# The last layer norm of a two-layer decoder step: tokens from 256 on turned to rows by a diagonal product, with mean and offset as a two-row product

## The reference

```python
def _layernorm(x, g, b):
    xf = x.astype(jnp.float32)
    mu = jnp.mean(xf, axis=-1, keepdims=True)
    var = jnp.mean(jnp.square(xf - mu), axis=-1, keepdims=True)
    y = (xf - mu) * lax.rsqrt(var + LN_EPS) * g.astype(jnp.float32) + b.astype(jnp.float32)
    return y.astype(x.dtype)
...
        yp = _layernorm(ALPHA * yp + 0.5 * _swiglu(yp, ffn2_wi[l], ffn2_wo[l]), ln_g[l, 2], ln_b[l, 2])
        ys = _layernorm(ALPHA * ys + 0.5 * _swiglu(ys, ffn2_wi[l], ffn2_wo[l]), ln_g[l, 2], ln_b[l, 2])
```

## Time and profile before

| | us |
|---|---|
| median of 3 runs (1842.55 to 1844.22) | 1843.87 |
| the profiled execution, its own time | 1845.71 |
| the span of its trace | 1843.9 |
| last product of the down projection ends, from the span's start | 1822.3 |
| from there to the end of the span | 21.6 |

### The profile page before, as it was taken

One profiled execution on the slowest core, in us unless ns is written; L12 is line 12 of the kernel. 1 busy time (PEld: TensorE's weight loads), 2 busy tenths in 40 slices (PEclk: granted clock), 3 DMA queues, 4 the chain that ended last, 5 costly groups with the idle time before them and its releaser, 6 DMA issues.

```text
span 1843.9 us, 35847 instructions
## 1 busy us (share of the span) xinstructions
PE 1766.2 (96%) x14078; PEld 1692.4 (92%) x14078; DVE 1455.5 (79%) x2188; ACT 932.3 (51%) x1464; POOL 422.9 (23%) x312
## 2 busy tenths in 40 slices
PE   7999999999997798999999999999999899999997
PEld 7999999986964488999999989999999799999996
DVE  5988887675988537988887599888876898887875
ACT  4455563353357736555562375555523475556333
POOL 3100044271220546000043230000542320002430
PEclk9999999999999999999999999999999999999999
DMA  5663423236210242343323324343323223433231
GB/s 167 193 200 96 114 87 103 87 100 140 54 55 1 61 123 70 92 114 104 101 92 98 109 69 111 94 114 103 98 83 118 57 56 106 114 102 104 81 103 47
DMA packets 275473, 180.73 MB, mean 98 GB/s; under 512 B 9367, under 2 KB 271903, under 8 KB 274846
## 3 DMA queue, kind: packets, MB, share of 16 engines
q1 hardware_dynamic: 266071, 158.50, 30.1%
q0 software_dynamic: 2144, 13.04, 2.0%
q10 hardware_dynamic: 7150, 7.70, 1.8%
HBM read 169.56 MB, written 8.08 MB: 96 GB/s over the span
## 4 chain that ended last, share of the span: by engine, by line
PE 74%; DVE 16%; ACT 6%; issue 3%; DMA 1%; POOL 0%; SPq 0%; ACTq 0%; DVEq 0%; POOLq 0%
PE ps L1372 41%; PE ps L1251 15%; PE ps L1435 9%; PE ps L1495 2%; DVE w_lo L1956 2%; PE ps L1500 1%; DVE q_lo L2643 1%; ACT xf L752 1%; ACT xh L750 1%; ACT p_t L887 1%; PE ps L1272 1%; DVE w_lo L2536 1%; ACT sc L865 1%; DVE q_sum L2720 1%; DVE xf L2006 1%
## 5 line engine op out<-in xcount | busy, mean ns | idle before, releaser
L2807 POOL TENSOR_TENSOR hl<-hid_all,hh 128x520 fp32r<-128x520 f32 x56 | 98.1, 1784 | 748.6 <-ACT hh L1111 748.6
L1041 ACT CAST w_hi<-w_sum 128x1024 fp32r<-128x1024 f32 x160 | 168.0, 1050 | 114.4 <-DVE w_sum L2518 107.0
L2536 DVE TENSOR_TENSOR w_lo<-w_sum,w_hi 128x1024 fp32r<-128x1024 f32 x160 | 194.4, 1217 | 4.5 <-ACT w_hi L1041 4.5
L1251 PE MATMUL ps<-hh,w_hi 128*128 128x260 f32 x896 | 191.7, 284 | 2.0 <-DVE w_lo L1956 2.0
L1251 PE MATMUL ps<-hh,w_lo 128*128 128x260 f32 x896 | 189.2, 282 | 0.0
L1372 PE MATMUL ps<-t_hi,w_hi 128*128 128x260 f32 x640 | 161.6, 284 | 0.7 <-DVE w_lo L2536 0.3
L1372 PE MATMUL ps<-xh,w_hi 128*128 128x260 f32 x640 | 159.9, 282 | 0.8 <-DVE w_lo L2536 0.8
L1372 PE MATMUL ps<-t_hi,w_lo 128*128 128x260 f32 x640 | 160.6, 283 | 0.0
L1372 PE MATMUL ps<-xh,w_lo 128*128 128x260 f32 x640 | 159.4, 283 | 0.0
L1251 PEld LDWEIGHTS ps<-hh,w_hi 128*128 128x128 f32 x896 | 145.3, 188 | 2.9 <-issue 2.7
L1251 PEld LDWEIGHTS ps<-hh,w_lo 128*128 128x128 f32 x896 | 145.6, 188 | 0.2
(11 more groups left out here) (376 smaller groups left out, 5234.7 us busy)
## 6 DMA issues: line engine op xcount, KB each, us to landing
w_raw<-in_ffn_wi_dram SPq DMA_DIRECT2D x176, 512.0 KB
w_raw<-in_ffn_wo_dram SPq DMA_DIRECT2D x16, 1024.0 KB
w_raw<-in_ffn_wo_dram SPq DMA_DIRECT2D x32, 512.0 KB
w_raw<-in_ffn_wo_dram SPq DMA_DIRECT2D x16, 768.0 KB
w_raw<-in_attn_w_in_dram SPq DMA_DIRECT2D x8, 1024.0 KB
keys_scratch<-key_half POOLq DMA_DIRECT2D x2, 2048.0 KB, 8.5
w_raw<-in_attn_w_o_dram SPq DMA_DIRECT2D x4, 1024.0 KB
x_in<-in_x_prompt_dram ACTq DMA_DIRECT2D x4, 512.0 KB, 9.9
```

The lines of the kernel that those rows point to most:

```text
L1041: nc.scalar.copy(blocks(st, j)[1][0][:, x], w_sum[:, c % 2, x]).then_inc(s_sums_hi, 1)
L1251: mm = nc.tensor.matmul(ps[0:mc, bank + 2 * m + h, 0:HT], w[:, k, m, 0:mc], x(k)[:, h * HT:(h + 1) * HT], start=first and k == 0 and w is ...
L2536: nc.vector.tensor_tensor(lo[:, x], w_sum[:, (st.chunk + j) % 2, x], hi[:, x].bitcast(F32), ALU.subtract).then_inc(s_sums_lo, 1)
L2807: nc.gpsimd.tensor_tensor(hl[:, k, :], hid_all[:, k, :], hh[:, k, :].bitcast(F32), ALU.subtract).then_inc(s_hl, 1)
```

## The change

Tokens 0 to 255 keep their path (subtract, multiply, gain and offset, transposes), now on 256 columns. Tokens 256 to 519 are no longer normalised in `xf`. With x a token's row before the norm, m its mean, s the root of its variance plus epsilon, g and b gain and offset, the output is (x g - m g + s b) / s. It is made piece by piece in PSUM:

- `scaled(i, q)`: four products with the raw `xf` tile as the stationary operand and `gain_diag` (a diagonal 128 x 128 matrix of the gain) as the moving one give x g, already turned to rows of tokens.
- `centred(i, q)`: one product with two rows, `token_rows` (-m and s, 2 x 128) stationary and `gain_rows` (g and b, 2 x 512) moving, is added in the same PSUM bank.
- The copy out multiplies by 1/s, one value for each partition (`token_stat`).

The three groups i = 2, 3, 4 each take 128 tokens; group 4 is the last 128 tokens, of which the last 32 partitions are copied out and the last 8 stored. Mean and mean square come from `token_moments`: for each group one product of the sum (stationary) with a single column of `mean_ones`, so that they stand one token to a partition, 128 x 3. DVE and ACT make m, s and 1/s on these 128 x 3 values, PE turns the pairs (-m, s) to two rows by three transposes, and DVE copies them into `token_rows`. `gain_diag` is written by ACT (eight 128 x 128 copies with a scale) after the last weights of the down projection have been split, into freed weight space, and SP loads `gain_rows` there in two transfers. `first_output` goes, `stats` of half 1 goes, and `variance` and `normalise` and `affine` of half 1 go.

```diff
-            for n in range(2, len(Y_ACT)):
+            for n in range(len(Y_ACT)):
                 output(n)
...
+            def final_tail(n, st, first_free):
+
+                order = (range(KD), range(KD))
+                act.wait_ge(s_lo, st.chunk + KF + 10 + 3)
+                for d in range(KD):
+                    x = nc.scalar.activation(gain_diag[:, d, :], ident, ACT.Copy, scale=gain(n, d))
+                x.then_inc(s_col_root, 1)
+                warm(ACT.Sqrt)
...
+            def scaled(i, q):
+
+                for d in range(4):
+                    nc.tensor.matmul(ps[:, Y_BANK[i, q], d * P:(d + 1) * P], xf[:, 4 * q + d, y_tokens(i)], gain_diag[:, 4 * q + d, :],
+                                     start=d == 0, stop=False, skip_group_check=True)
+
+            def centred(i, q):
+
+                nc.tensor.matmul(ps[:, Y_BANK[i, q], :], token_rows[:, (i - 2) * P:(i - 1) * P], gain_rows[:, q * 512:(q + 1) * 512],
+                                 start=False, stop=True, skip_group_check=True).then_inc(s_tr, 1)
...
+                pe.wait_ge(s_in, 16 * 8)
+                pe.wait_ge(s_col_var, 4)
+                centred(2, 0)
+                centred(2, 1)
+                centred(3, 0)
+                scaled(3, 1)
+                centred(3, 1)
+                pe.wait_ge(s_y_act, 1)
+                scaled(4, 0)
+                centred(4, 0)
+                pe.wait_ge(s_y_dve, 1)
+                scaled(4, 1)
+                centred(4, 1)
...
+                last_residual(0)
+                last_sums(st, 0, 0)
+                last_sums(st, 0, 1)
+                variance(st, eps, 0)
+                normalise(st, 0, order, 0, KD - 2, 2 * P)
+                last_residual(1)
+                last_sums(st, 1, 0)
+                last_sums(st, 1, 1)
+                normalise(st, 0, order, KD - 2, KD, 2 * P)
...
-                nc.vector.tensor_copy(dst, src).then_inc(s_y_dve, 1)
+                dst, src, rstd = y_half(i, q)
+                if i < 2:
+                    nc.vector.tensor_copy(dst, src).then_inc(s_y_dve, 1)
+                else:
+                    dve.wait_ge(s_col_root, 3)
+                    nc.vector.tensor_scalar(dst, src, rstd, None, ALU.mult).then_inc(s_y_dve, 1)
```

More of the change, by code:

```diff
@@ L743, in root, with affine @@
                 nc.scalar.activation(moment(1, h), moment(1, h), ACT.Sqrt).then_inc(s_rstd, 1)
-            def affine(n, st, h, split, order, begin, end):
+            def affine(n, st, h, split, order, begin, end, tokens=None):
+                tokens = tokens or cols(h)
                 for at_ in range(begin, end):
@@ L1930, in _ @@
             left()
[L1931 to L1938, removed]
         @block.vector
@@ L1993, in last_sums, with normalise @@
                 ins.then_inc(s_total, 1)
-            def normalise(st, h, order, begin, end):
+            def normalise(st, h, order, begin, end, count=HT):
+                tokens = slice(h * HT, h * HT + count)
                 n = {}
@@ L1998, in normalise @@
                     if at_ < end:
-                        x = xf[:, order[h][at_], cols(h)]
-                        n[at_] = step(nc.vector.tensor_tensor(x, x, moment(0, h), ALU.subtract))
+                        x = xf[:, order[h][at_], tokens]
+                        n[at_] = step(nc.vector.tensor_tensor(x, x, moment(0, h)[:, 0:count], ALU.subtract))
                     if at_ == begin + 1:
@@ L2004, in normalise, with final_tail @@
                         done(n[at_ - 1])
-                        x = xf[:, order[h][at_ - 1], cols(h)]
-                        nc.vector.tensor_tensor(x, x, moment(1, h), ALU.mult).then_inc(s_t, 1)
+                        x = xf[:, order[h][at_ - 1], tokens]
+                        nc.vector.tensor_tensor(x, x, moment(1, h)[:, 0:count], ALU.mult).then_inc(s_t, 1)
+            def final_tail(st, eps, last_residual):
+                order = (range(KD), range(KD))
+                last_residual(0)
[7 more added lines that the diff above has]
+                normalise(st, 0, order, KD - 2, KD, 2 * P)
+                mean, square, var, inv = (token_stat[:, n, :] for n in range(4))
+                dve.wait_ge(s_col_sum, 2)
+                nc.vector.tensor_scalar(token_pair[:, :, 0], ps[:, 7, 0:3], -1.0, None, ALU.mult).then_inc(s_col_var, 1)
+                done(step(nc.vector.tensor_copy(mean, ps[:, 7, 0:3])))
+                done(step(nc.vector.tensor_tensor(square, mean, mean, ALU.mult)))
+                done(step(nc.vector.scalar_tensor_tensor(var, ps[:, 7, 3:6], eps, square, ALU.add, ALU.subtract)))
+                nc.vector.tensor_scalar(var, var, eps, None, ALU.max).then_inc(s_col_var, 1)
+                dve.wait_ge(s_col_var, 2)
+                nc.vector.reciprocal(inv, var).then_inc(s_col_var, 1)
+                dve.wait_ge(s_col_sum, 3)
+                nc.vector.tensor_copy(token_rows[:], ps[0:2, 7, 0:3 * P]).then_inc(s_col_var, 1)
             def tail(st, eps, last_residual, nxt, early):
```

100 lines of the change are left out of this document (83 added, 17 removed).

## The result

| | before | changed | forecast |
|---|---|---|---|
| median, us | 1843.67 (13 runs) | 1847.78 (13 runs) | 1840.6 (range 1838.6 to 1844.0) |
| range of the runs, us | 1840.05 to 1847.13 | 1844.65 to 1848.99 | |
| ratio to before, 95% interval | | 1.0020 (1.0012 to 1.0027) | 0.998 |
| span of the profiled execution, us | 1843.9 | 1846.1 | 1840.6 |
| end of the down projection to the end of the span | 21.6 | 24.7 | 18.3 |

The last row is the one to work with, and is called the tail from here on. A difference of whole times holds this variation, the tail doesn't.

A forecast was written before the change was run, and what follows sets the result against it. Late stores behind a serial chain set the old end; PE becomes the bound. From 1822.3, PE ends at 1837.05, copy 1837.75, issue 1837.8, landing 2.4 and end 0.4 give 1840.6 us, 3.3 less; range 1838.6 to 1844.0.

The forecast's parts named there:

- PEclk 1.00 throughout: Sign of a right forecast: PE at full clock from 1822.3 to about 1837 us, behind the down projection.
- the clock falls and stays low to the end: Rival: PE's path from 1826.8 us takes twice as long, +10.1 us, 1850.7 us, slower; chance 0.05.
- The weaker rival, low for 6.8 us and back: Rival: the clock falls behind the down projection as before, losing 3.4 us; 1844.0 us, no gain; chance 0.09.
- -3.3 as forecast: Forecast gain at the end of the span: 1840.6 us, 3.3 us less than 1843.9.
- the faster landing: Last store, 32 KB to HBM: 2.4 us (2.0 to 3.0) from issue, plus 0.4 us to the span's end.
- the prediction's own rule: In the clock rivals, PE work takes twice as long at PEclk 0.50, so half of a low stretch is lost.
- the rival of 0.53 us: Rival: `centred` products cost 0.53 us instead of 0.87, six times 0.34 less; 1838.6 us; chance 0.05.
- the one-column products: Six PE products turning the sums into moments, after three pieces of `scaled`: 0.20 us each, 1.2 us, ending at 1826.1.
- the chain on 128 x 3 values: Small operations, root, pair transposes and DVE copies before the first `centred`, until about 1828.9 us; PE was to cover them.
- the last piece of cover before `last_residual(1)`: Three more tiles ahead of it cost DVE 2.0 us of 2.86 us idle; free, with 0.8 us left.
- the stores spread: Store groups released near 1829.7, 1830.4, 1831.8 and 1834.5 us, 1.2 us each, leaving the queue empty for the last store.
- without gaps: Sign of a right forecast: PE busy without gaps from 1822.3 to about 1837 us.

The follow-up runs named there:

- with 128 rows: Changed kernel with the two rows of `centred` operands repeated 64 times over 128 rows, pair scaled; median 1840.26 us, ratio to before 0.9984; again 1839.81 us, 0.9987.
- the stretch of 120 transposes: Kernel before with gapless PE work added behind its end: runs of 512-column products on 128, 2, 32 and 64 rows, then 120 transposes; 1960.85 us.
- 64-row version: Changed kernel with the pair and the gain and offset rows repeated over 64 rows; median 1839.99 us, ratio to before 0.9974; again 1842.72 us, 0.9996.

## Why the prediction was wrong

Measured from the end of the down projection, in us:

| | forecast | changed kernel | with 128 rows |
|---|---|---|---|
| transposes begin | 4.5 | 4.6 | 4.6 |
| first `centred` begins | 6.8 | 6.9 | 6.9 |
| PE ends | 14.7 | 21.7 | 14.8 |
| SP issues the last store | 15.5 | 22.5 | 15.7 |
| the span ends | 18.3 | 24.7 | 17.9 |

**The step that failed** is the forecast's "PEclk 1.00 throughout": the products of `centred` are summed at the full clock, and the rival "the clock falls and stays low to the end" is put aside. Its mechanism was named, with "5.2 of the 7.8 us are products that use two rows of the array" as the reason for it, and given a chance of 0.05. It is what happened: PEclk 0.50 from 1831 on, and 12.05 us for the six pieces behind it where 5.2 (six times 0.87) had been forecast. The reason set against it, that the clock had come back at 1833.3 with nothing but sixteen transposes done, was a true reading of the earlier trace rows, and the stretch of 120 transposes bears it out; but it answers the half of the rival that concerns transposes, and says nothing of products on two rows. The trace of before has no product on two rows, which the prediction says where it costs `centred`, and then bounds its duration only, never its effect on the clock. But it has products on eight rows, and right behind them, at 416.8 us, a fall under a PE without a gap; the prediction read the clock at the end of the trace alone. The weaker rival, low for 6.8 us and back, had the greater chance (0.09) because it repeated what the trace of before had shown.

**The price** put on this rival, +10.1 us, was for a clock low from 1826.8 on. It fell at 1831, four microseconds later, and its moment is partly chance: the traces differ by 2.7 us in it, which is worth half of that in time. The part from there to PE's end takes 12.05 us; the same products take 6.44 us in the 64-row version at the full clock and 5.27 us in the 128-row one. So 5.6 us are the clock's and 1.2 us the cost of changing between few and all rows, which the prediction does not have. The sum against before: -3.3 as forecast, +5.6 and +1.2, +0.1 in the first three `centred`, +0.2 in small delays elsewhere, -0.6 for the faster landing: +3.2, and the tails give 24.7 - 21.6 = +3.1. By the prediction's own rule 12 us at the low clock lose 6 us of a gain of 3.3, which gives a small loss, as measured. That the medians lie 4.1 us apart, 1 us more than the tails, is variation ahead of the tail.

**The rest held.** `scaled` at 0.87 us a piece (24 records in 2.8 us ahead of the moments, the latency of the last included); `centred` at 0.87 us by columns (2.77 us for three, 0.86 with 128 rows), so the rival of 0.53 us is out; the one-column products 0.24 us instead of 0.20; no wait of PE for the chain on 128 x 3 values; the last piece of cover before `last_residual(1)` 0.9 us (0.8 forecast); PE the bound and the stores spread. PE did idle for 0.67 us ahead of the transposes, where the prediction's list of signs says "without gaps"; its own times (1826.1 and 1826.8) have that gap. With 128 rows the tail is 17.9 us, 0.4 less than forecast: the store takes 2.2 us from issue to the end of the span, in the changed kernel and in the 128-row one alike, where 2.8 was taken, and 0.2 us are lost ahead of its issue.

The Trainium skill, TensorE: Matmul & The Clock Gate, section "What's actually happening", has the clock follow how busy PE has been. Here PE was busy for all of 1830.50 to 1831.00 and of every window behind it, and the clock fell; it also fell twice in the gapless stretches. With busy read as the busy time of the profile, the forecast would have stood by that rule; the measurement decides. The same page's "Part 4: PE-mode transpose", which the prediction had weighed and set aside, says that transposes do not count as activity. 120 of them over 13.3 us, all at PEclk 1.00, disagree with it, so it was right to set it aside, and wrong to let the rows of the product go with it.

## What to carry to other kernels

A product on two rows costs PE the time of one on 128 (and 0.2 us at each change between the two), but it does not hold the clock: where such products fill microseconds of a stretch that sets the end, give them all rows, by repeating theirs with a scale or by zeros. Here that turned 1.0020 of before into 0.9984 and 0.9987, with no cost that the tail shows, and it is the version to keep, faster than both kernels. And where an edit brings a kind of instruction that the trace has never shown, look through the whole trace for what the clock does around its nearest relatives, bound what it does to the clock as well as its duration, and price the low clock for the whole stretch behind it.

## What was not expected of the hardware

- A busy PE can lose its full clock: 2-row products did it in the kernel (PEclk 0.50 from 1831 on, PE at 100%) and in a bare stretch, 32-row products in a bare stretch only. Neither 64-row products nor transposes did it, in a bare stretch or in the tail. Under a gapless PE the clock also fell at 416.8 us of the kernel before, behind products on 8 rows.
- Zeros count as work: 126 zero rows of 128 held the clock as well as real ones (17.9 us tail for both; one trace with zeros).
- Each change between products on fewer rows (2, 32 or 64) and on 128 costs about 0.2 us at the full clock: 1.09 and 1.05 us where 128 rows throughout take 0.89 and 0.86. The cause was not looked into.
